# A fused decoder block: where ScalarE copies a projection out and splits two gate and up chunks, at the begin of the feed-forward

## The reference

```python
x = x + rmsnorm(m @ w_out[i], mix_post_norm[i])
h = rmsnorm(x, ffn_pre_norm[i])
f = (jax.nn.silu(h @ w_gate[i]) * (h @ w_up[i])) @ w_down[i]
x = x + rmsnorm(f, ffn_post_norm[i])
e = rmsnorm(p[i] @ w_ple_proj[i], ple_norm[i])
x = x + jax.nn.sigmoid(x @ w_ple_gate[i]) * e
```

## Time and profile before

| What | Value |
|---|---|
| Median of 3 runs | 1935.26 us (1933.86 to 1935.46) |
| The profiled execution's own time | 1933.96 us |
| Its span in the trace | 1932.2 us |
| PE busy | 1919.8 us, 99% of the span |
| DVE, ACT and POOL busy | 64%, 47% and 28% |
| Chain that ended last | PE 96%, DVE 2%, ACT 1% |
| Granted TensorE clock | full in all 40 slices |

### The profile page before, as it was taken

The page is one execution under the profiler, slowest core; times in us unless marked ns, Lnnn a source line. Parts: engine busy times, 40 slices in busy tenths (PEclk is TensorE's granted clock), DMA queues, the critical chain, the costliest instruction groups (busy, mean ns, idle before and its releaser), DMA issues.

```text
span 1932.2 us, 23713 instructions
## 1 busy us (share of the span) xinstructions
PE 1919.8 (99%) x9248; PEld 1602.8 (83%) x9248; DVE 1234.4 (64%) x1711; ACT 904.2 (47%) x1322; POOL 538.8 (28%) x403
## 2 busy tenths in 40 slices
PE   9999999999999999999999999999999999999998
PEld 7788888888888888888888888888888888888887
DVE  7778757348136745454546857658666676766758
ACT  7556544324245443424255444434455555444435
POOL 2434452340505344453532000000333341000000
PEclk9999999999999999999999999999999999999999
DMA  5312466566423313122225656365322226746553
GB/s 167 96 47 79 122 131 157 136 145 144 99 88 98 121 66 109 66 90 77 93 66 162 169 150 176 106 194 121 96 87 87 87 66 185 182 123 174 125 181 87
DMA packets 164690, 229.70 MB, mean 119 GB/s; under 512 B 4784, under 2 KB 108976, under 8 KB 164464
## 3 DMA queue, kind: packets, MB, share of 16 engines
q1 hardware_dynamic: 148192, 195.24, 33.1%
q0 software_dynamic: 16096, 32.01, 9.5%
q10 hardware_dynamic: 304, 1.12, 0.2%
HBM read 223.23 MB, written 4.72 MB: 118 GB/s over the span
## 4 chain that ended last, share of the span: by engine, by line
PE 96%; DVE 2%; ACT 1%; issue 0%; DMA 0%; POOL 0%; SPq 0%; ACTq 0%
PE ps L1162 30%; PE ps L1164 30%; PE ps L1163 30%; PE ps L1377 1%; PE ps L1347 1%; PE ps L1387 1%; PE ps L1386 1%; PE ps L1364 0%; PE ps L1903 0%; DMA o_buf<-in_x 0%; DVE x L3348 0%; PE ps L1201 0%; DVE hn_lo L3352 0%; ACT hn_hi L2145 0%; ACT w_hi L2056 0%
## 5 line engine op out<-in xcount | busy, mean ns | idle before, releaser
L1162 PE MATMUL ps<-hn_hi,w_hi 128*128 128x512 f32 (+1 forms) x1540 | 601.3, 390 | 1.2 <-DVE hn_lo L3546 0.5
L1164 PE MATMUL ps<-hn_hi,w_lo 128*128 128x512 f32 (+1 forms) x1540 | 593.1, 385 | 0.0
L1163 PE MATMUL ps<-hn_lo,w_hi 128*128 128x512 f32 (+1 forms) x1540 | 592.8, 385 | 0.0
L1012 POOL TENSOR_TENSOR w_lo<-raw,w_hi 128x512 fp32r<-128x512 f32 x244 | 344.1, 1442 | 508.6 <-ACT w_hi L2048 508.6
L1162 PEld LDWEIGHTS ps<-hn_hi,w_hi 128*128 128x128 f32 x1540 | 289.4, 188 | 62.9 <-issue 6.1
L1164 PEld LDWEIGHTS ps<-hn_hi,w_lo 128*128 128x128 f32 x1540 | 289.3, 188 | 58.3
L1163 PEld LDWEIGHTS ps<-hn_lo,w_hi 128*128 128x128 f32 x1540 | 289.6, 188 | 57.2 <-issue 1.7
L1162 PE MATMUL ps<-w_hi,hid_hi 128*128 128x512 f32 x616 | 240.0, 390 | 0.7 <-DVE hid_lo L3097 0.7
L1164 PE MATMUL ps<-w_hi,hid_lo 128*128 128x512 f32 x616 | 239.7, 389 | 0.0
L1163 PE MATMUL ps<-w_lo,hid_hi 128*128 128x512 f32 x616 | 239.6, 389 | 0.0
L2092 ACT ACTIVATE w_hi<-raw 128x1024 fp32r<-128x1024 f32 x112 | 116.3, 1056 | 207.8 <-PE ps L1164 205.4
(11 more groups left out here) (400 smaller groups left out, 2935.3 us busy)
## 6 DMA issues: line engine op xcount, KB each, us to landing
raw<-in_mlp_w SPq DMA_DIRECT2D x56, 1024.0 KB, 5.4
raw<-in_ret_w_in SPq DMA_DIRECT2D x24, 1024.0 KB, 5.2
aux<-in_mlp_w POOLq DMA_DIRECT2D x16, 1024.0 KB, 8.9
raw<-in_att_w_in SPq DMA_DIRECT2D x12, 1024.0 KB, 5.8
raw<-in_w_gate SPq DMA_DIRECT2D x11, 1024.0 KB, 5.4
raw<-in_w_up SPq DMA_DIRECT2D x11, 1024.0 KB, 5.4
raw<-in_w_down SPq DMA_DIRECT2D x9, 1024.0 KB, 5.1
raw<-in_ret_w_out SPq DMA_DIRECT2D x8, 1024.0 KB, 5.1
```

The costliest lines, as they stand in the source:

```text
L1012: ins = pool.tensor_tensor(w_lo[:, slot, at], raw[:, slot, at], w_hi[:, slot, at].bitcast(F32), ALU.subtract)
L1162: pe.matmul(o, hi, rhs_hi, start=start, stop=False, skip_group_check=True)
L1163: pe.matmul(o, hi, rhs_lo, start=False, stop=False, skip_group_check=True)
L1164: return pe.matmul(o, lo, rhs_hi, start=False, stop=stop, skip_group_check=True)
```

## The change

Only ACT's program is changed, in two places. `copy_e(2)` (the copy of PROJ's third group) and `ffn_up_hi(0, 1)` (the high part of the second chunk) now stand ahead of the loop over the new tiles of x, the high part first. `copy_e(3)` moves up from the third tile to the first. And the high part of the third chunk, `ffn_up_hi(0, 2)`, stands one square further ahead.

```diff
             copy_e(0)
             rsqrt(N_POST, D)
             copy_e(1)
+            ffn_up_hi(0, 1)
+            copy_e(2)
             for n, t in enumerate(FFN_ORDER):
                 act.wait_ge(s["post_x"], 2 * n + 2)
                 gained_hi(N_FFN, t, ("ffn_pre_norm", t))
                 if n < 2:
                     square(N_FFN, n, x[:, t, :])
                 if n == 0:
-                    copy_e(2)
-                if n == 2:
-                    ffn_up_hi(0, 1)
                     copy_e(3)
             for n, t in enumerate(FFN_ORDER):
-                if n == 4:
+                if n == 3:
                     ffn_up_hi(0, 2)
                 if n >= 2:
                     square(N_FFN, n, x[:, t, :])
             ffn_up_hi(0, 3)
```

## The result

| | Before | Changed |
|---|---|---|
| Median (22 runs each) | 1934.54 us (1933.58 to 1935.46) | 1937.51 us (1935.98 to 1939.74) |
| Ratio | | 1.0016, 95% interval 1.001 to 1.0022 |
| Profiled execution, own time | 1933.96 us | 1937.82 us |
| Its span | 1932.2 us | 1936.0 us |

The account below looks back on a forecast made before the run. TensorE, busy for 99% of the span, was taken as the bound, so only its waits count. 2.53 + 1.04 - 0.47 = +3.1 us on the median 1935.26 gave 1938.4 us, range 1935.8 to 1941.2.

Parts of the forecast that it names:

- rival 2: The clock falls in PE's gap before the old tiles, replacing the tiles' lateness; +3.9 to +5.7 us, chance 13%.
- Term 1: At the old tiles, PE restarts later because group 2's copy stands behind the second chunk's split on ACT; +2.53 us.
- Term 2: At the new tiles, DVE slowed by POOL makes low parts late, so PE waits at the third and fourth; +1.04 us.
- Term 3: At chunk 2, the sooner third split removes PE's wait for the low part; -0.39 us and -0.08 us.
- The granted clock should stay full: Sign expected in the trace: TensorE keeps its full clock, 2.4 GHz, despite a gap of 3.04 us.
- That the third split had to move too: At chunk 2, leaving the third split one square later would start it some 4 us later and make PE wait again.
- part 1: The second chunk's split moved ahead of group 2's copy on ACT; PE idle 3.04 us in one piece, +2.53 us.
- The sums over squares: In the middle of chunk 2, sums end at 255.7 and PE comes at 256.8; cover 1.1 us, costed at nothing.
- Rival 2's price: Clock fall in the gap, costed as 2.53 + 1.8 - 0.47 = 3.9 us, the 1.8 taken from matmuls at the program's begin.
- Rivals 1, 3 and 4: Tiles not late, +2.1 us, 13%; split let go early, -0.9 us, 4%; third PE wait, +4 to +5 us, 8%.

Follow-up runs that it names:

- e3: The changed kernel with its two moved lines swapped, copy of group 2 first, then the second chunk's split; +2.61 us over the kernel before, ratio 1.0012.
- e4: The changed kernel with 11 surplus matmuls on PE ahead of its wait for the copy of group 2; +3.15 us over before, ratio 1.0017.
- e1: The kernel before with only the third chunk's split one square sooner; -1.00 us against before, ratio 0.9996.
- e2: The changed kernel with the third chunk's split put back where it was before; +3.28 us over before, ratio 1.002.
- e5: The changed kernel with PE's product on the mixer's output ahead of its wait for the emptied pair of banks; +2.41 us over before, ratio 1.0014.
- e10: The changed kernel run again, with no further edit; +3.18 us over before, ratio 1.0014.
- e8: The changed kernel with surplus matmuls in the gap and POOL's second-chunk low part held until the third new tile; one run, +3.45 us over before.

## Why the prediction was right, point by point

The time, the side and the size were right: +3.1 us forecast, +2.97 and +3.18 measured. Of the 0.9 us between 1938.4 and 1937.51, 0.7 lies in the starting value, 1935.26 from three runs where 22 gave 1934.54. The path to it was right in its first step. In the middle one it was not the forecast's mechanism that ran but rival 2's, which had 13%: the forecast named a dip of the clock as a sign of being wrong, and the clock dipped. The last step's gain came, but not by the edit that was meant to bring it. So the nearness of the sum to the time is in part luck, and by the trace's stretch, 3.51 us, it was 0.4 short.

- **Term 1, the copy behind a split that waits for the last group: +2.53 us.** Right. The restart came 2.63 us later, counted from the first sum over squares (225.28 - 214.27 against 222.98 - 214.60). The 0.1 us too few is the hand-over from PE to ACT, 0.11 us from the last matmul's end at 222.14 to 222.25, which I had left at 0.03. e3 shows that the split causes the gap: with the copy ahead of it the gap is gone.
- **Term 2, the tiles late by POOL: +1.04 us.** As a mechanism right, but not what PE did. "The granted clock should stay full" was the step that failed. The gap made the clock fall for some 3 us, and PE was 1.61 us behind its pace when it came to the tiles, so that it found each one there. In e4, where the clock stays full, the waits are those of the forecast and cost 1.07 us. The pattern of DVE's rows moved as I had said, to 0.05 us between POOL's start and the first slow instruction (1.54 us in the changed kernel, 1.58 forecast).
- **Term 3, the low part at chunk 2: -0.47 us.** The sign was right, the size too small. A wait of 0.39 us by the profile's idle time cost 0.62 us of pace, since idleness is counted only from the modelled end of the last matmul: starts lie 0.77 us apart there (247.36 to 248.13) where 0.23 is the pace, and the matmul behind the wait takes 0.08 us more. With the sum over squares 0.06 us late, that makes about 0.7 us, as e1 shows (0.72).
- **That the third split had to move too** for the changed kernel was wrong. I put its loss at a new wait of PE. e2 has no such wait, so behind part 1 the gain of term 3 comes without the edit. The forecast had PE at chunk 2 0.7 us too early (251.1 against 251.49, in a trace that starts 0.33 us sooner) and put the split 0.2 us too late.
- **The sums over squares** were in time, with 1.8 us to spare where I had 1.1.
- **Rival 2's price**, 2.53 + 1.8 - 0.47 = 3.9 us, was high by 0.4. The trace gives 2.63 + 1.61 - 0.73 = 3.51. That the 1.8 came so near is in part luck: it was drawn from a slow pace at the program's begin, where the windows view gives a granted clock of 1.00 from 0 to 4 us, so those rows don't show a fall of the clock. That two mechanisms gave nearly one time made the forecast safer than its reasons were. The gap plus clock stand for 3.5 us by the trace, the gap plus late tiles for 2.9.
- **Rivals 1, 3 and 4** are out. Tile waits show as soon as the clock is full, ACT did wait for the last group, and no third wait came.

The rule of the Trainium skill that I had weighed (TensorE: Matmul & The Clock Gate, "Why this matters for your kernels") asks for no idle gaps over about 3 us between bursts of matmuls. These traces agree with it: the clock fell at a gap of 3.15 us in all three, and it stayed full behind 2.27 us (e3) and behind 0.51. With my own gap of 3.04 us at the rule's edge, 13% for the fall was too little.

## What to carry to other kernels

On an engine that runs in strict order, look up what a moved instruction waits for, not only how long it takes. Here a split of 1.9 us, moved ahead of a ready copy, held the engine for 4.45 us until an event that the copy didn't need. When a wait of the bound engine is taken away, compute who is late next before counting the gain. In e3 the whole gap of 3 us went and in e5 all but 0.34 us of it, and 2.6 and 2.9 us of loss stayed, since the next operands were late by nearly as much. And a gap of PE near 3 us should be priced with a fall of the clock, here 1.5 to 1.6 us over the next 24 matmuls, less what PE would have waited behind them anyway, here 1 us.

## What the runs showed of the hardware

- The same gap of 3.15 us did not bring the fall of the clock at the same point. In the changed kernel two matmuls started at full pace behind it (225.28, 225.59) before the spacing rose, and in e10 four. In e2 the clock fell some 0.3 us before PE went on.
- At half clock a matmul of 512 columns started every 0.43 us, against 0.227 at full.
- DVE's instructions with two SBUF operands took 1.5 to 1.8 us while POOL subtracted, against 0.7 to 0.75 us, and this followed POOL when it was moved by 6.7 us (e8).
- A wait on PE costs more than its idle time in the profile: 0.62 us for a wait that shows as 0.39.
